# The shared rotary key of a latent attention, projected beside another group's values

## What is computed

```python
h = rms_norm(x, g_mix[l])
proj = h @ w_in[l]
c_q, c_kv, k_r, qkv_b, qkv_c, gate_logits = jnp.split(proj, IN_SPLITS, axis=-1)
y_a = mla_mixer(c_q, c_kv, k_r, g_q[l], g_kv[l], w_uq[l], w_ukv[l])
...
    k_rope = apply_rope(k_rope, cos, sin)          # 32 columns, shared by the 8 heads of branch A
    s = (jnp.einsum('bqhd,bkhd->bhqk', qn, k_nope, preferred_element_type=jnp.float32)
         + jnp.einsum('bqhr,bkr->bhqk', qr, k_rope, preferred_element_type=jnp.float32)) * scale
```

## Time and profile before

| | |
|---|---|
| median of 3 runs | 3301.63 us (3300.11 to 3301.95) |
| span of the profiled execution | 3299.3 us |
| TensorE busy | 3266.6 us, 99% |
| VectorE busy | 1611.1 us, 49% |
| ScalarE busy | 1245.0 us, 38% |
| GpSimd busy | 348.4 us, 11% |
| DMA | 295.22 MB, mean 89 GB/s |

### The profile page before, as it was taken

The page is one execution under the profiler, slowest core; times in us unless marked ns, Lnnn a source line. Parts: engine busy times, 40 slices in busy tenths (PEclk is TensorE's granted clock), DMA queues, the critical chain, the costliest instruction groups (busy, mean ns, idle before and its releaser), DMA issues.

```text
span 3299.3 us, 38708 instructions
## 1 busy us (share of the span) xinstructions
PE 3266.6 (99%) x15604; PEld 2662.9 (81%) x15604; DVE 1611.1 (49%) x2325; ACT 1245.0 (38%) x2007; POOL 348.4 (11%) x316
## 2 busy tenths in 40 slices
PE   8999999999999999999999999999999999999998
PEld 7886788888887867888888877878888888888887
DVE  5565544443345574444343544344533359763234
ACT  4564323322335563233323332223422248642222
POOL 3121000100011220001000211002100032130001
PEclk9999999999999999999999999999999999999999
DMA  4221222222222211222223222222222322322232
GB/s 151 67 75 56 76 96 96 96 96 96 96 96 80 84 43 64 96 96 96 96 97 100 97 87 86 93 86 67 94 100 92 102 84 90 103 84 97 95 102 71
DMA packets 83231, 295.22 MB, mean 89 GB/s; under 512 B 9616, under 2 KB 12016, under 8 KB 82928
## 3 DMA queue, kind: packets, MB, share of 16 engines
q1 hardware_dynamic: 80352, 283.78, 25.8%
q0 software_dynamic: 2704, 8.98, 0.8%
HBM read 289.55 MB, written 3.18 MB: 89 GB/s over the span
## 4 chain that ended last, share of the span: by engine, by line
PE 94%; DVE 3%; POOL 1%; ACT 1%; issue 1%; DMA 0%; SPq 0%; ACTq 0%; DVEq 0%; POOLq 0%
PE bank L2659 28%; PE bank L2661 28%; PE bank L2660 28%; PE bank L2920 3%; PE bank L2928 2%; PE bank L3063 1%; PE bank L2873 1%; POOL xs L1275 1%; PE bank L2888 1%; PE bank L3053 1%; DVE w_lo L1966 0%; PE bank L2899 0%; PE bank L2941 0%; PE bank L2740 0%; PE bank L2750 0%
## 5 line engine op out<-in xcount | busy, mean ns | idle before, releaser
L1966 DVE TENSOR_TENSOR w_lo<-raw_ring,w_hi 128x1024 fp32r<-128x1024 f32 x530 | 666.6, 1258 | 1104.8 <-ACT w_hi L1486 1104.2
L2659 PE MATMUL bank<-h_hi,w_hi 128*128 128x512 f32 (+1 forms) x2752 | 1061.5, 386 | 14.4 <-DVE w_lo L1966 11.4
L2661 PE MATMUL bank<-h_hi,w_lo 128*128 128x512 f32 (+1 forms) x2752 | 1052.0, 382 | 0.0
L2660 PE MATMUL bank<-h_lo,w_hi 128*128 128x512 f32 (+1 forms) x2752 | 1051.7, 382 | 0.0
L1486 ACT ACTIVATE w_hi<-raw_ring 128x1024 fp32r<-128x1024 f32 x530 | 561.6, 1060 | 1159.6 <-PE bank L2661 1092.6
L2659 PEld LDWEIGHTS bank<-h_hi,w_hi 128*128 128x128 f32 x2752 | 518.1, 188 | 119.5 <-issue 15.9
L2661 PEld LDWEIGHTS bank<-h_hi,w_lo 128*128 128x128 f32 x2752 | 518.0, 188 | 101.2
L2660 PEld LDWEIGHTS bank<-h_lo,w_hi 128*128 128x128 f32 x2752 | 518.3, 188 | 99.6 <-issue 1.2
L2659 PE MATMUL bank<-act_hi,w_hi 128*128 128x512 f32 (+1 forms) x1336 | 507.3, 380 | 0.3 <-DVE act_lo L1979 0.3
L2661 PE MATMUL bank<-act_hi,w_lo 128*128 128x512 f32 (+1 forms) x1336 | 504.7, 378 | 0.0
L2660 PE MATMUL bank<-act_lo,w_hi 128*128 128x512 f32 (+1 forms) x1336 | 504.6, 378 | 0.0
(11 more groups left out here) (216 smaller groups left out, 2550.6 us busy)
## 6 DMA issues: line engine op xcount, KB each, us to landing
raw_ring<-weights SPq DMA_DIRECT2D x530, 512.0 KB, 3.3
arena<-rpb POOLq DMA_DIRECT2D x16, 320.0 KB, 3.5
xs<-x_t SPq DMA_DIRECT2D x8, 256.0 KB, 6.3
out_t<-xs SPq DMA_DIRECT2D x16, 128.0 KB, 1.8
arena<-block SPq DMA_DIRECT2D x1, 1024.0 KB, 9.1
arena<-o_nat POOLq DMA_DIRECT2D x2, 512.0 KB, 3.6
arena<-ret POOLq DMA_DIRECT2D x4, 256.0 KB, 3.1
o_nat<-arena POOLq DMA_DIRECT2D x2, 384.0 KB, 3.1
```

The costliest lines, as they stand in the source:

```text
L1966: nc.vector.tensor_tensor(w_slot(w_lo, u), raw_slot(u), f32(w_slot(w_hi, u)), ALU.subtract) \
L2659: nc.tensor.matmul(out, lhs[0], rhs[0], start=first, stop=False)
L2660: nc.tensor.matmul(out, lhs[0], rhs[1], start=False, stop=False)
L2661: return nc.tensor.matmul(out, lhs[1], rhs[0], start=False, stop=last)
```

## The change

The group m = 3 of the input projection goes. The 32 columns of the rotary key are appended, once, to each weight piece of the B,0 values, which are 288 columns wide now. Each value tile then holds the key of its 128 tokens in columns 256 to 287; ScalarE writes them four times side by side, with the row scale, into tile `KRAW`, ahead of the copy of the values. Behind m = 3 of the B,1 dense part TensorE transposes the four tiles (`kt`), ScalarE copies the result back to `KRAW`; behind m = 4 TensorE multiplies by the rotation matrix (`krot`), and VectorE writes the product with the sine to `kr` and that with the cosine to `KRAW`. GpSimd adds both after its transfers for the outputs of B,0. `KRAW` is a tile of its own, the arena grows by one. ScalarE's wait for the sum ahead of C,0's attention is gone.

```diff
@@ -35,7 +35,7 @@
 SPLIT_SLOTS = 3
-ARENA_TILES = 31
+ARENA_TILES = 32
 BIAS_BLOCKS = 5
...
@@ -46,9 +46,10 @@
 GROUPS = [("C", 0), ("B", 0), ("B", 1), ("B", 2), ("A", 0), ("A", 1), ("C", 1)]
-CIN = (2, 0, 1, 3)
+CIN = (2, 0, 1)
 X_LOADS = 8
 TURNS = {("A", 1): [("B", 2)]}
+KEY_TURN, KEY_ROT = ("B", 1, 3), ("B", 1, 4)
 HALF = S // 2
...
@@ -192,8 +193,7 @@
         for m in CIN:
-            c = cols(m * P, P) if m < 3 else cols(A_COLS - MLA_ROPE, MLA_ROPE) * GH
-            out.append(((l, "cin", m, k), w_in, k, c))
+            out.append(((l, "cin", m, k), w_in, k, cols(m * P, P)))
     for br, g in GROUPS:
...
@@ -213,7 +213,8 @@
         else:
-            many(out, (l, "v", br, g), w_in, range(KD), cols(at + 2 * width + g * GW, GW))
+            many(out, (l, "v", br, g), w_in, range(KD),
+                 cols(at + 2 * width + g * GW, GW) + cols(A_COLS - MLA_ROPE, MLA_ROPE))
     for kind, m, b in gate_steps():
...
@@ -573,7 +574,6 @@
                 p.add(("sum", "q", l), "norm")
-                p.add((l, "krot"), "dve")
             if m == 3:
...
@@ -617,6 +617,10 @@
                     attend(*GROUPS[j - 1], m)
+                if (br, g, m) == KEY_TURN:
+                    p.add((l, "kt"), "act")
+                elif (br, g, m) == KEY_ROT:
+                    p.add((l, "krot"), "dve")
             for group in TURNS.get((br, g), []):
...
@@ -948,8 +955,8 @@
         SC_RING, PB_RING, PT_RING = {"B": 2, "C": 4}, 4, 4
-        CRAW, KRAW, T2 = 22, 21, 14
-        SQC, KT1, KT2 = 16, 19, 20
+        CRAW, KRAW, T2 = 22, 31, 14
+        SQC = 16
         CQ_ACT = 8
...
@@ -1331,9 +1338,6 @@
                     bias_load(l, h)
-                pool.wait_ge(krope_terms, l + 1)
-                nc.gpsimd.tensor_tensor(kr[:, :], tile(KT1), tile(KT2), ALU.add).then_inc(krope_sum, 1)
-                pool.wait_ge(krope_sum, l + 1)
                 pool.wait_ge(cs_ready, 2 * l + 2)
...
@@ -1368,6 +1372,9 @@
                         .then_inc(b0_back, 16)
+                pool.wait_ge(krope_terms, l + 1)
+                nc.gpsimd.tensor_tensor(kr[:, :], kr[:, :], tile(KRAW), ALU.add).then_inc(krope_sum, 1)
+                pool.wait_ge(krope_sum, l + 1)
                 for m in range(4):
...
@@ -1685,6 +1692,14 @@
                                 continue
+                            before(key)
+                            wait_acc(act, key)
+                            if (l, t) == (1, 0):
+                                act.wait_ge(krope_sum, l)
+                            rope = bank(key)[:, GW:GW + MLA_ROPE].rearrange("p (c d) -> p c d", c=1)
+                            nc.scalar.activation(tile_t(tile(KRAW), t).rearrange("p (c d) -> p c d", c=GH),
+                                                 rope.to_broadcast([P, GH, MLA_ROPE]), ACT.Identity,
+                                                 scale=inv8[:, t:t + 1])
                             copy_out(key, V[:, t, :], func=ACT.Identity, width=GW, scale=inv8[:, t:t + 1])
...
@@ -1799,14 +1814,14 @@
                             attend(l, *GROUPS[j - 1], m)
+                        if (br, g, m) == KEY_TURN:
+                            copy_out((l, "kt"), tile(KRAW))
                         if (br, g) == ("C", 1) and m in LATENT_DENSE:
                             latent_end(l, "A", LATENT_DENSE[m], 1, 1)
                         if (br, g) == ("B", 0) and m in NEAR_DENSE:
                             latent_end(l, "C", NEAR_DENSE[m], 0, 1)
                     for group in TURNS.get((br, g), []):
                         turned(l, group)
-                    if j == 0:
-                        act.wait_ge(krope_sum, l + 1)
                     attend(l, br, g, "main")
...
@@ -2363,10 +2378,7 @@
                     b = group((l, "cin", m))
-                    if m < 3:
-                        nc.vector.tensor_tensor(latents[m], b[:, :], rb[:, :], ALU.mult).then_inc(dve_freed, 1)
-                    else:
-                        nc.vector.tensor_tensor(tile(KRAW), b[:, :], rb[:, :], ALU.mult).then_inc(dve_freed, 1)
+                    nc.vector.tensor_tensor(latents[m], b[:, :], rb[:, :], ALU.mult).then_inc(dve_freed, 1)
                 for j, (br, g) in enumerate(GROUPS):
...
@@ -2403,10 +2415,10 @@
                             latent_end(l, "C", NEAR_DENSE[m], 0, 1)
-                        if j == 0 and m == 2:
-                            b = group((l, "krot"))
-                            nc.vector.tensor_tensor(tile(KT2), b[:, :], c("sin_a"), ALU.mult).then_inc(dve_freed, 1)
-                            nc.vector.tensor_tensor(tile(KT1), tile(KRAW), c("cos_a"), ALU.mult) \
+                        if (br, g, m) == KEY_ROT:
+                            b = group((l, "krot"), step=True)
+                            nc.vector.tensor_tensor(kr[:, :], b[:, :], c("sin_a"), ALU.mult).then_inc(dve_freed, 1)
+                            nc.vector.tensor_tensor(tile(KRAW), tile(KRAW), c("cos_a"), ALU.mult) \
                                 .then_inc(krope_terms, 1)
...
@@ -2998,7 +3007,11 @@
                             norm_sum("q", l, SQC, 2)
-                            wait_freed(pe, (l, "cin", 3))
+                        if (br, g, m) == KEY_TURN:
+                            wait_freed(pe, (l, "v", "B", 0, NT - 1))
+                            turn((l, "kt"), lambda t: tile_t(tile(KRAW), t))
+                        elif (br, g, m) == KEY_ROT:
+                            wait_freed(pe, (l, "kt"))
                             b = start_group((l, "krot"))
```

More of the change, by code:

```diff
@@ L905, in c, with tile_t @@
             return fixed[:, a:a + w]
+        def tile_t(ap, t):
+            return ap[:, t * P:(t + 1) * P]
         def tiles(n, count, width=S):
@@ L1165, in weighty @@
             return not (key[0] in ("sum", "spread", "rs", "rout", "ryt") or
-                        key[1] in ("krot", "rot", "yt", "vt", "A", "B", "C"))
+                        key[1] in ("kt", "krot", "rot", "yt", "vt", "A", "B", "C"))
         start_pos, done_pos, piece_pos, unit_end, pos = {}, {}, {}, {}, 0
@@ L1756, in first_inputs @@
                     if k % 2 == 0:
-                        before((0, "cin", 3), 1, piece_pos[(0, "cin", 3), 1] + 1 if k > 4 else 0)
+                        before((0, "cin", CIN[-1]), 1, piece_pos[(0, "cin", CIN[-1]), 1] + 1 if k > 4 else 0)
                     if k > 1:
@@ L2715, in tokens_abreast @@
                             mm.then_inc(acc_ready, 1)
-            def tile_t(ap, t):
-                return ap[:, t * P:(t + 1) * P]
             def stride_t(ap, t):
```

## The result

| us | before | after |
|---|---|---|
| median (lowest to highest) | 3301.1 (3300.11 to 3301.95) | 3322.93 (3318.12 to 3323.85) |
| runs | 5 | 5 |
| ratio, 95% interval | | 1.0061 [1.0049, 1.0073] |

The change makes the kernel 21.8 us slower. The forecast was 3305.7 with a range up to 3311: the direction of the likeliest case was right, the size was off by a factor of five (4.1 us forecast).

The account below looks back on a forecast made before the run. TensorE's instruction stream was taken as the bound. Per layer -5.44 + 1.28 + 0.8 + 4.9 + 0.4 + 0.1 = +2.0 us, +4.1 for two, took the median from 3301.63 to 3305.7 us, range 3297 to 3311.

Parts of the forecast that it names:

- (d): B,0 values: third weight unit split too late, TensorE stops 18 matmuls in; +4.9 us a layer, bounds 0 and 7.3.
- (e): B,0 attention: two splits queue on VectorE before the second scores, which are taken later; +0.4 us a layer, 0 to 1.14.
- (a): Input projection: the fourth group's 24 matmuls go; -5.44 us a layer.
- (c): Four transposes turn the key back, the rotation moves at no net cost, the stream breaks twice more; +0.8 us a layer.
- (b): B,0 values: 96 matmuls widen from 256 to 288 columns; +1.28 us a layer.
- The rival that no stop arises: B,0 values: third unit split in time, layer at -2.9 us, time 3295.9 us; chance 0.12.
- (f): A,0: shifted units put one more split on VectorE before the rotation product; +0.1 us a layer, up to 1.0.
- (g): Moved VectorE and GpSimd work and layer 0's earlier sum of squares cost nothing; the latter at most 1.4 us once.
- Rival one: Clock falls to 1.2 GHz after the stop in the values, 1.35 us a layer, 3308.4 us; chance 0.26.
- Doubling the stretch: Half speed after the stop in the values lasting twice as long as at the kernel's start; 3311 us.

Follow-up runs that it names:

- early_one: Changed kernel, third unit of the B,0 values split once its slot is free, and one split, not two, ahead of the last value tile's copy: 3294.78 us.
- pack_early_one: Kernel before, B,0 value pieces packed 288 wide (256 used), third unit split once its slot is free, one split ahead of the last tile's copy: 3303.41 us.
- one: Changed kernel, ahead of the last value tile's copy only one of the two free units split, the other at its old place: 3307.68 us.
- pack: Kernel before, B,0 value pieces packed 288 columns wide so they fill three units, only 256 used, TensorE's work unchanged: 3319.56 us.
- wait1: Kernel before, one more VectorE product (result unused) ahead of the mask of B,0's third scores in each layer: 3308.37 us.
- wait2: Kernel before, two more VectorE products (results unused) ahead of the mask of B,0's third scores in each layer: 3309.79 us.
- early: Changed kernel, third unit of the B,0 values split as soon as its slot is free, ahead of the last rotation's work: 3303.44 us.

## Why the prediction was wrong, step by step

The runs let the whole difference be laid out. The parts of the path are read from first matmuls: values of B,0, first group of B,1, first group of A,0.

| us, layer 0 / layer 1 | read as | |
|---|---|---|
| the stop (d) | 4.85 / 4.71 | forecast 4.9 |
| half rate behind it | 1.7 / 1.5 | value stage 20.08 / 19.74 against 13.52 / 13.54 in `early_one`, less the stop |
| later scores (e) | 0.8 / 0.8 | 2.46 from second to third scores, 1.66 in `early_one` |
| second fall, up to B,1 | 5.4 / 5.5 | value start to B,1 start 38.68 / 38.45 against 25.92 / 25.94, less the rows above |
| second fall, in B,1 | 1.6 / 1.3 | B,1 start to A,0 start 88.66 / 88.38 against 87.09 / 87.06 |
| sum | 14.3 / 13.8 | 28.1 in all; after and `early_one` are 28.15 apart by their medians, 28.6 by the spans of the profiled executions |

The forecast of 3305.7 was 17.2 us too low. The second fall, which it did not have, is 13.8 us of that, the first, which it had only as a rival, 3.2.

**(a), right.** The group is gone. The values begin 5.42 us earlier (107.05 against 112.47), but that holds two more things: the profiled execution starts its first matmul 0.43 us later (8.95 against 8.52), and the rotation has left C,0, see (c).

**(b), right in size.** In `early_one` the value stage takes 13.52 us against 11.96: +1.56, forecast 1.28. The spacing is the 0.133 us that was forecast; the rest is the small step at a new unit that `pack_early_one` shows (0.32 us between two matmuls at 109.47).

**(c), a little high.** From B,1's start to A,0's start the path grows by 1.42 us in `early_one` (87.09 against 85.67). In C,0 the stretch from the rotation to the spreading of the row scales gets 0.84 us shorter: it took from 51.62 to 58.05, and takes from 46.88 to 52.47 with the same 24 dense matmuls. Net 0.6, forecast 0.8.

**(d), right in mechanism, place and size:** 18 matmuls in, 4.85 and 4.71 us against 4.91 and 4.89. The rival that no stop arises has fallen.

**(e), right as a wait, wrong as a price.** The splits queue as described (126.56, then the scores at 128.90), and TensorE's wait grows from 0.32 to 0.96 us: +0.64, forecast +0.4 and inside its bounds. **This is the step that failed:** it was priced by its length alone, between 0 and 1.14 us. Its true price in the changed kernel is 7.6 us a layer (15.2 us, `one` against after), because the clock falls behind it. I had thought of a fall only behind the long stop.

**(f), low.** A,0 begins 2.74 us earlier in `early_one` than before (219.91 against 222.65), its first scores only 2.13 us earlier (233.09 against the 235.22 of the earlier trace rows): 0.6 us lost, forecast 0.1, up to 1.0. TensorE waits 0.47 us ahead of these scores, in every kernel with the new packing and in both layers; before, it did not. VectorE's rotated queries end at 232.67 in `early_one`, but the profile puts the wait down to ScalarE's copy of A,0's values; which of the two ends it was not tested.

**(g), right** so far as it can be seen: TensorE doesn't wait for the sum of squares of layer 0 (GpSimd is done at 25.75 us, forecast near 25). Not forecast was a gain: the old kernel waited 0.94 us at 1015.46 in layer 1, and `early_one` waits 0.17 there. It happens in one layer only, and I did not look for its cause. The clock held behind that wait in all five profiles that have it (the kernel before, `pack`, `pack_early_one`, `wait1`, `wait2`).

Without stop and falls the layer was forecast at -2.9 us, 3295.9 in all. `early_one` gives 3294.78, 6.0 us below the kernel before, where 5.7 was forecast. Part of that is luck: (b) was 0.3 us too low and (c) 0.2 too high, (f) was 0.5 too low while (e) is not in `early_one`, and the 0.8 us of layer 1 were not foreseen.

**Rival one, the clock.** Its mechanism was the right one and its chance, 0.26, too low, though the rule of the Trainium skill beside it spoke for it; its size was wrong in two ways. Behind the stop the fall cost 1.7 and 1.5 us, close to the 1.35 worked out from the start. But it was put in one place only, and its length was carried over from a start that runs into dense 128x512 matmuls. In the attention of B,0 the clock stayed at the 1.2 GHz level from 132 us to 149.2, which takes in the first 3.5 us of the dense group from 145.73 on. TensorE was busy without a break all the while (17.10 us of 17.10), with small matmuls up to 145.73; so it is not further waiting that kept the clock down, and the runs don't show what did. Doubling the stretch gave an upper end of 3311 to the whole; `one`, which has the first fall alone, came out at 3307.68, within the range. The second fall lies outside every case that I had. The Trainium skill has a place that bears on it ("TensorE: Matmul & The Clock Gate", section "A second HAM failure mode: psum-queue depth-cycling"): short idle times between groups of matmuls, if frequent, can make the clock fall and rise again. The trace agrees in part: idle times of 0.96, 0.17 and 0.35 us stand ahead of the fall at 132 us, but then the clock falls once and stays down for 17 us, and how often TensorE pauses was not varied. I had weighed the section ahead of it, on long waits, and read 0.32 us of waiting in the old kernel as harmless, without asking what 1 us there would do.

What stays open: why an equally long wait lets the clock fall in one layer or one run and not in another (`early`: layer 0 and not layer 1; `pack`: neither in the profiled run, at 1.10 us), and what ends a long fall: that all six have about the same length speaks against the dense work of B,1 as the sole cause. The runs show how often, not by what. Nor is a wait of a microsecond always needed. In the profile of the kernel before, the clock falls for 3.4 us in the part that the change doesn't touch, behind 16 matmuls of 128x1 with 0.20 us of idle time between them:

```profile
1895.50:1899.00 3.50, 3.50 (x10) 2.76 (x9) 0.00 (x0) 0.00 (x0) 1.60 (x4) 0.51 0.77 287
```

The changed kernel, `early_one` and `pack` show this fall too, those of `early`, `one`, `pack_early_one`, `wait1` and `wait2` don't. By the spacing of its matmuls it costs some 1.6 us when it comes, and either side of a comparison can have it.

## What to carry to other kernels

Price a new wait of TensorE by what runs behind it, not by its length alone: in a stretch of small matmuls with waits of its own, 0.6 us more of waiting cost 6 to 7 us beyond itself whenever the clock fell, since it stayed down for some 17 us; in dense work the clock held behind six stops of up to 1.9 us. Widening a packed weight piece changes how many units a loop holds at once: check, at every turn of the loop, which slot the next split waits for and what it then stands ahead of on VectorE. A change that does save work can lose nearly five times as much by two splits a layer in the wrong place (28.1 us against 6.0); both could be moved, and then it paid.

## What the runs showed of the hardware

- A wait of 0.96 to 1.04 us in the attention of B,0 was followed by the 1.2 GHz level in both layers of the changed kernel's profile, in one layer of those of `early` and `wait1`, and in neither layer of `pack`'s at 1.10 us; in both layers after 1.77 us (`wait2`, profiled run); and not after the 0.15 to 0.32 us of `one`, `early_one` and the kernel before.
- In dense 128x512 work the clock held behind all stops up to 1.91 us, fell behind two of six between 2.24 and 2.97 us, and behind all twenty from 3.15 us on. After a stop of 2.43 us the fall came some 1.5 us after the restart (1812.98 to 1814.47), not with it.
- A fall cost 1.1 to 2.9 us in dense work, 1.5 to 2.0 us in the values of the changed kernel and of `one`, and 6 to 7 us in the attention.
- The long falls lasted about 17 us each, six of six, though TensorE was busy nearly all of that time; a fall of 3.4 us came behind matmuls of 128x1 with 0.20 us of idle time, in four of the nine profiles without added stops in dense work.
